# Moving half a gate projection ahead of four transposes, and a modulation product behind an output product, in two mixer layers

## The reference, cut to what matters

```python
for l in range(DEPTH):                       # DEPTH = 2
    h = x @ w_in[l]
    (hg_q, hg_f, hg_i, hg_gate, mla_cq, mla_ckv, mla_kr, mla_gate, mem_q, mem_gate) = jnp.split(h, ...)
    y_hg  = _hgrn2_group(hg_q, hg_f, hg_i, ...)   # gated recurrence, done here in 8 levels per half
    y_mla = _mla_group(...)                       # softmax(q k^T) v, 8 heads
    y_mem = _memory_group(...)                    # 4 heads on the memory tokens
    y = jnp.concatenate([y_hg * silu(hg_gate), y_mla * silu(mla_gate), y_mem * silu(mem_gate)], -1)
    x = _layernorm(ALPHA * x + y @ w_out[l], ...)
...
mod = jnp.einsum('bd,de->be', jax.nn.silu(c), w_ada) + b_ada   # 1024 -> 6144, of the third block
```

## Time and profile before

| | us |
|---|---|
| median of 3 runs | 1421.64 |
| lowest and highest | 1419.9, 1423.33 |
| the profiled execution, its own time | 1422.7 |
| its span in the profile | 1420.9 |
| PE busy (matmul) | 1274.7 (90%) |
| POOL busy | 652.0 (46%) |
| DVE busy | 815.0 (57%) |

### The profile page before, as it was taken

The page is one execution under the profiler, slowest core; times in us unless marked ns, Lnnn a source line. Parts: engine busy times, 40 slices in busy tenths (PEclk is TensorE's granted clock), DMA queues, the critical chain, the costliest instruction groups (busy, mean ns, idle before and its releaser), DMA issues.

```text
span 1420.9 us, 17530 instructions
## 1 busy us (share of the span) xinstructions
PE 1274.7 (90%) x6312; PEld 786.6 (55%) x6312; DVE 815.0 (57%) x1681; ACT 412.2 (29%) x1030; POOL 652.0 (46%) x643
## 2 busy tenths in 40 slices
PE   9999999999999999999998899958877778787876
PEld 8877686548876686559566546523323333333332
DVE  1766377341656377450438756789797654454545
ACT  1532344211333333121323333322312231212123
POOL 0656667332537666524003454444745445544540
PEclk9999999999999999999999999979989998999999
DMA  9544334365453354354637999999999999999995
GB/s 377 199 165 177 119 142 187 124 256 196 156 186 149 119 216 167 144 225 167 234 122 303 423 412 410 421 421 421 421 421 422 421 422 422 422 422 420 422 422 208
DMA packets 53888, 407.84 MB, mean 287 GB/s; under 512 B 6165, under 2 KB 8618, under 8 KB 11306
## 3 DMA queue, kind: packets, MB, share of 16 engines
q0 software_dynamic: 36864, 268.45, 45.7%
q1 hardware_dynamic: 15850, 137.23, 25.1%
q10 hardware_dynamic: 1088, 1.05, 0.3%
HBM read 404.58 MB, written 1.07 MB: 285 GB/s over the span
## 4 chain that ended last, share of the span: by engine, by line
PE 39%; DMA 24%; DVE 7%; issue 4%; POOL 3%; ACT 2%; ACTq 0%; DVEq 0%; POOLq 0%
PE pj L693 13%; PE bank L1119 10%; DMA ring<-in_peer_uv,vM 7%; DMA yT<-in_peer_uv,vM 7%; PE pj L729 5%; PE pj L708 4%; DMA hv<-in_peer_uv,vM 4%; DMA more_rows<-in_peer_uv,vM 3%; DMA qM<-in_peer_uv,vM 3%; PE pj L989 2%; POOL more_rows L607 1%; DVE tri L1871 1%; PE bank L653 1%; POOL mod_part L608 1%; DMA qvE<-in_peer_uv,vM 1%
## 5 line engine op out<-in xcount | busy, mean ns | idle before, releaser
L693 PE MATMUL pj<-xT,ring 128*128 128x256 f32 (+1 forms) x1568 | 320.1, 364 | 0.9 <-ACT hv L1276 0.4
L693 PEld LDWEIGHTS pj<-xT,ring 128*128 128x128 f32 x1568 | 277.7, 191 | 37.2 <-issue 2.9
L607 POOL TENSOR_SCALAR more_rows<-more_rows,lbt 128x256 f32<-128x256 f32 x168 | 175.0, 1041 | 16.4
L641 POOL DMA_INDIRECT ring<-in_peer_uv,vM x101 | 119.6, 1184 | 110.4 <-PE bank L1119 97.6
L605 POOL TENSOR_SCALAR mod_part<-more_rows,lbt 128x256 f32<-128x256 f32 x24 | 26.9, 1122 | 252.7 <-issue 110.3
L729 PE MATMUL pj<-ring,yT 128*128 128x512 f32 x320 | 141.3, 595 | 0.0
L1336 ACT ACTIVATE rope<-vM 128x4 f32<-128x4 f32 (+3 forms) x84 | 17.1, 204 | 406.9 <-DVE big L1871 324.1
L608 POOL TENSOR_TENSOR mod_part<-mod_part,more_rows 128x256 f32<-128x256 f32 x168 | 126.8, 755 | 14.0
L1119 PE MATMUL bank<-ring,causal 128*128 128x512 f32 x200 | 98.1, 628 | 17.7 <-ACT causal L1344 17.7
L1119 PE MATMUL bank<-ring,tri 128*128 128x512 f32 x204 | 96.4, 611 | 17.7 <-ACT tri L1344 17.7
L729 PEld LDWEIGHTS pj<-ring,yT 128*128 128x128 f32 x320 | 59.5, 190 | 69.4 <-issue 69.2
(11 more groups left out here) (369 smaller groups left out, 2112.2 us busy)
## 6 DMA issues: line engine op xcount, KB each, us to landing
ring<-in_units SPq DMA_DIRECT2D x44, 2048.0 KB, 9.8
more_rows<-in_w_ada SPq DMA_DIRECT2D x24, 1024.0 KB, 5.0
ring<-in_units SPq DMA_DIRECT2D x2, 1536.0 KB, 8.5
ring<-in_peer_uv,vM POOLq DMA_INDIRECT x101, 23.4
memT<-in_mem SPq DMA_DIRECT2D x2, 512.0 KB, 5.0
ring<-in_units SPq DMA_DIRECT2D x1, 1024.0 KB, 8.3
xT<-in_x_turned SPq DMA_DIRECT2D x1, 1024.0 KB, 10.1
x<-in_x SPq DMA_DIRECT2D x1, 1024.0 KB, 17.4
```

The costliest lines, as they stand in the source:

```text
L607: do(g.tensor_scalar(mod_w[:, c, :], mod_w[:, c, :], silu_c[:, c:c + 1], None, ALU.mult))
L641: pool.indirect_dma_start(row_slot[k], None, d["peer_uv_2"], bass.IndirectOffsetOnAxis(ap=expert[:, t, j:j + 1], axis=0))\
L693: ins = nc.tensor.matmul(pj[s][0:n, 2 * m + first:2 * m + stop], ring[:, slot, at:at + n], act[:, c, first:stop], start=(c == 0), stop=(c ...
```

## The change

Four edits of the same two kinds, one of each in each layer's string. First, `P0 GMa AD Y0 GMb` becomes `GMa P0 AD GMb Y0`: each half of the gate projection goes ahead of a small product that it stood behind. Second, `AD O0u` becomes `O0u AD`: the ninth modulation product of the layer (`AD8`, and `AD20` in layer 1) goes behind the output product of the second tile. In the DVE string, which both layers share, the same piece goes behind the two steps `Da18 Db18` (the preparation of recurrence level 8).

```diff
-PE_ORDER: ... L02 AD S2 P0 GMa AD Y0 GMb L03 Q1a L04 Q1b S3
+PE_ORDER: ... L02 AD S2 GMa P0 AD GMb Y0 L03 Q1a L04 Q1b S3
...
-            O0t L17 Y9 AD O0u LD L18 O2t HO2 HO3 AD HN2 AD O2u LD HN3 O3t AD O1t O3u O1u
+            O0t L17 Y9 O0u AD LD L18 O2t HO2 HO3 AD HN2 AD O2u LD HN3 O3t AD O1t O3u O1u
...
-DVE_ORDER: ... L15 L16 Db17 L17 AD Da18 Db18 L18 Y9 HO2 AD HO3 HN2 AD HN3 AD LN
+DVE_ORDER: ... L15 L16 Db17 L17 Da18 Db18 AD L18 Y9 HO2 AD HO3 HN2 AD HN3 AD LN
```

More of the change, by code:

```diff
@@ L50 @@
 N_MOD_PIECES = N_MOD * D_MODEL // MOD_COLS
-PE_ORDER = ["""MKa MKb C VEC F0 N Q0 LD UQ KR F1a UK LD UV S0 F1b L01 S1 L02 AD S2 P0 GMa AD Y0 GMb L03 Q1a L04 Q1b S3
+PE_ORDER = ["""MKa MKb C VEC F0 N Q0 LD UQ KR F1a UK LD UV S0 F1b L01 S1 L02 AD S2 GMa P0 AD GMb Y0 L03 Q1a L04 Q1b S3
             P1 L05 Y1 LD AD I0a P2 LD L06 LD S4 S5 P3 I0b Y2 AD AD Y3 P4 MV Y4 L07 P5 G0a L08 LD Y5 LD AD G0b MQ LD
             AD HO0 S6 HO1 HN0 L11 GEa AD P6 S7 GEb S8 HN1 L12 LD I1 Y6 L13 P7 P8 S9 L14 Y7 G1a G1b P9 Y8 L15 LD L16
-            O0t L17 Y9 AD O0u LD L18 O2t HO2 HO3 AD HN2 AD O2u LD HN3 O3t AD O1t O3u O1u""",
-            """MKa Xt MKb Xu MKc C F0 N Q0 LD UQ KR F1a UK LD UV S0 F1b L01 S1 L02 AD S2 P0 GMa AD Y0 GMb L03 Q1a L04 Q1b S3
+            O0t L17 Y9 O0u AD LD L18 O2t HO2 HO3 AD HN2 AD O2u LD HN3 O3t AD O1t O3u O1u""",
+            """MKa Xt MKb Xu MKc C F0 N Q0 LD UQ KR F1a UK LD UV S0 F1b L01 S1 L02 AD S2 GMa P0 AD GMb Y0 L03 Q1a L04 Q1b S3
             P1 L05 Y1 LD AD I0a P2 LD L06 LD S4 S5 P3 I0b Y2 AD AD Y3 P4 MV Y4 L07 P5 G0a L08 LD Y5 LD AD G0b MQ LD
             AD HO0 S6 HO1 HN0 L11 GEa AD P6 S7 GEb S8 HN1 L12 LD I1 Y6 L13 P7 P8 S9 L14 Y7 G1a G1b P9 Y8 L15 LD L16
-            O0t L17 Y9 AD O0u LD L18 O2t HO2 HO3 AD HN2 AD O2u LD HN3 O3t AD O1t O3u O1u""",
+            O0t L17 Y9 O0u AD LD L18 O2t HO2 HO3 AD HN2 AD O2u LD HN3 O3t AD O1t O3u O1u""",
             """Xt BUt BKt Xu MT BUu BKu BQa BQb SK S0 S1 BVa S2 PL0 PL1 BVb P0 P1 S3 S4 Y0 S5 Y1 O1t P2 O0t P3 Y2 P4 Y3 P5 Y4
@@ L78 @@
     FP1 Da11 Da12 AD Db11 AD HO0 S6 L11 P6 HO1 HN0 Da13 Db12 Db13 S7 AD Da14 S8 P7 P8 HN1 Db14 L12 Y6 L13
-    Da15 Da16 S9 Da17 P9 Y7 Db15 Db16 L14 Y8 L15 L16 Db17 L17 AD Da18 Db18 L18 Y9 HO2 AD HO3 HN2 AD HN3 AD LN"""
+    Da15 Da16 S9 Da17 P9 Y7 Db15 Db16 L14 Y8 L15 L16 Db17 L17 Da18 Db18 AD L18 Y9 HO2 AD HO3 HN2 AD HN3 AD LN"""
 DVE_LAST = """Xu S0 S1 S2 PL0 PL1 N0 N1 S3 N2 S4 S5 N3 N4 Y1 N5 OMt Y5 NMt Zt Rt0 XP1 OMu H2t NMu D1 Zu D3 H2u D4 GT1
```

## The result

The changed kernel takes 1429.16 us (median of 5 runs, 1428.37 to 1430.36), beside 1422.19 us of before in the same session. The ratio is 1.0043, with a 95% interval of 1.0028 to 1.0058: slower by 6.1 us by the ratio and 7.0 by the two medians. The direction was forecast; the size was not. The forecast was +12.7 us.

A forecast was written before the change was run, and what follows sets the result against it. PE's order was taken to bound the layers, with POOL's chain rigid behind AD8. Layer 0 at +6.97 - 1.0 and layer 1 at +6.97 - 0.2 gave +12.7 us, 1434.4 us; range 1430 to 1438.

The forecast's parts named there:

- What bounds the kernel, and the sign: PE's order sets the layers' time; delaying AD8 and AD20 costs more than is gained; slower, chance 0.92.
- The first place: At P0 and GMa: 1.99 us gained in each layer, plus 1.65 for the clock in layer 0, together 5.63.
- How much of it survives: Of the gain at P0 and GMa, loads and POOL's pace leave 1.0 us in layer 0, 0.2 in layer 1.
- rival 2: The gain at P0 and GMa is kept whole, as loads and pieces come earlier: +8.3 us, 1429.9, chance 0.10.
- It is 34.97 us, all of it POOL and one load, with no slack: POOL's chain from AD8 to AD11 keeps its length, so AD11 moves by 6.97 us; layer 1 costed alike.
- This edit is worth nothing: Moving DVE's piece behind Da18 Db18 gains nothing; left in place, it would hold up level 8 for 7 us.
- The waits behind `AD8`: PE waits 3.6 us at AD10 and AD22, 2.4 for O3's load, some 2 at AD11 and AD23.
- rival 1: The clock falls behind AD11 or AD23: +1.65 us for one, +3.3 for both, 1436.0 to 1437.6, chance 0.14.
- The waits for POOL as listed: PE waits 2.6 us in layer 0 between 104 and 220, 1.7 at AD16; line 870 totals near 14.
- The signs of being wrong: AD11 less than 4 us later; I1 over 2 us earlier; a layer 1 end delay smaller in the total.
- the third sign: A delay at the end of layer 1 that is smaller in the total would mean the third block absorbs it.
- No change, and faster: Within 3 us of 1421.64, chance 0.05; or gain kept and delay fully hidden, 1416.0, chance 0.03.

## Why the prediction was wrong, point by point

- *What bounds the kernel, and the sign:* right. PE's order sets the layers, `AD8` releases POOL's last two pieces, and their chain ends in a wait of PE. +11.1 us for the second edit alone against 13.94 recorded. (The row of GB/s reads 410 to 423 from slice 22 on and 208 in the last slice, not 410 to 422 throughout; nothing hangs on it.)
- *The first place, 5.63 us of gain* (1.99 in each layer and 1.65 for the clock): right in size. `P0` has no wait, and `GMa` takes 7.07 us in both layers. The clock's share was one draw: with `P0` first, `GMa` ran slowed in 3 of 6 executions in layer 0 and in 5 of 6 in layer 1, by 1.0 to 1.7 us; with `GMa` first, in none of eight layers.
- *"How much of it survives", the step that failed.* I took 1.0 and 0.2 us; the trace has 3.6 and 1.3. The waits at `AD4` and `AD16` that limit it are of the kind forecast, but I had worked the limit from times at which the kernel before had its pieces ready, as if these could not move. They moved: the end of piece 7 from 117.16 to 113.99 us behind `AD0`, and that of piece 16 from 56.12 to 55.10 behind `AD12`. This is 3.6 us of the 6.1 missing. I had put the opposite case down as rival 2, with the full 5.63 kept, +8.3 us and a chance of 0.10. Of its two halves the runs bear out the first, that the pieces come earlier; the gain was not kept whole, and beside an unslowed `GMa` it is 1.0 to 1.2 us a layer. That the time comes out even below +8.3 is due to the next point.
- *"It is 34.97 us, all of it POOL and one load, with no slack":* the mechanism was right and the term mis-sized. It measured 33.71 and 33.78, since pieces 10 and 22 no longer run beside `Da18` and `Db18`. 2.5 us.
- *"This edit is worth nothing"*, of DVE's part: wrong for the same reason. By the run with DVE's old order it is what shortened the two pieces; the stall of level 8 that I had foreseen without it was there (4.56 us), and hidden.
- *The waits behind `AD8`:* 2.23 at `AD10` instead of 3.6, again 1.3 less for the piece. `O2u` then took 8.83 us, where 7.13 is usual: the granted clock averaged 0.68 and then 0.50 there. That fall was forecast as hidden, and hidden it was; it used up most of the wait for `O3`, 0.37 us instead of 2.4. Behind `AD11` and `AD23` the clock did not fall in this execution, so rival 1 was not met here, although the wait at `AD23` (2.46 us) was longer than those at `AD10` and `AD22` (2.23 each), behind which it fell. It was met once in the run with only the second edit: behind the 2.51 us at its `AD23` the granted clock averaged 0.50 between 626 and 628 us. How many of the changed kernel's other executions met it isn't known.
- *The waits for POOL as listed:* 2.6 us in layer 0 ahead of 220 and 1.7 at `AD16` were forecast, 1.03 (at `AD4`) and 0.95 came. The total of 14 was a slip, since its own parts add up to about 15.5; it measured 10.8.
- *The signs of being wrong.* Two of the three came. `I1` started at 216.57 and not 219.42, 2.85 us earlier, and this sign read rightly: the loads were not fixed by `AD0`. `AD11` started 2.75 us later than before, under the 4 us that I had named, and this sign misleads: PE waits there for POOL, for 1.90 us, so POOL's chain was the bound. The 4 us left no room for a larger gain kept at the first place and a shorter chain. Of the third sign, that the third block takes up a delay, the two traces give a hint (`AD23` came 7.2 us later, and the span grew by 5.7), but as shown above they can't settle it.
- *No change, and faster:* rightly unlikely. POOL was idle for 22.65 us ahead of piece 10, where 17.17 it had been and 23 were forecast.

Two rows of the clock in the changed kernel, for the stretches behind `AD10`:

```profile
282.80:285.00 2.20, 2.20 (x9) 1.09 (x5) 2.10 (x4) 0.00 (x0) 0.00 (x0) 0.68 0.75 190
285.00:287.00 2.00, 2.00 (x3) 0.72 (x3) 1.90 (x4) 0.00 (x0) 0.00 (x0) 0.50 1.06 446
```

0.50 is the lower level, 1.2 GHz.

## What to carry to other kernels

When a chain of GpSimd work is what others wait for, read the duration of its instructions as they stand against VectorE's, not only their sum. The same instruction at 0.92 and at 1.24 us in one trace says that its length is not its own, and a move on another engine can shorten or lengthen the chain (here by 1.3 us in a piece of 15). A limit worked out from the times at which something was ready before holds only if nothing that the change moves can act on what makes it ready.

A producer that stands idle waiting for one product of the bottleneck engine is a reason to move that product earlier rather than later, even if the product itself is 0.3 us long. Here some 7 us later cost 11.1 us over two layers, and 9 us earlier gained 1.7, all that PE had been waiting for.

## What the runs showed of the hardware that I had not expected

GpSimd's product of a tile with a column (128x256) took 0.92 us beside an idle VectorE, beside VectorE reading PSUM, and beside six maxima over one SBUF tile, and 1.24 us beside products of two SBUF tiles. VectorE's products took 6.02 us for six there, 1.00 each with their gaps, and the six maxima of equal size 4.29, or 0.72. The Trainium skill states this as a rule ("SBUF — State Buffer", Who interferes with whom): a VectorE instruction with two SBUF inputs contends with a GpSimd instruction that reads SBUF, while one with at most one SBUF input outside the two-port modes does not. The traces agree on both halves. I had not brought the rule to bear on the prediction, and it bears on both terms that were mis-sized.

A stall of 2.0 us ahead of `GMa` was followed by a slowed `GMa` in eight of twelve layers (8.03 to 8.76 us, beside 7.07), and the wait of 2.2 us at `AD10` and `AD22` by a slowed `O2u` in all four layers seen (8.83 us beside 7.13), while seven waits of 1.58 to 2.51 us at `AD11` and `AD23` were followed by a fall only once, behind the longest. So the length of a stall alone does not tell whether the clock falls.
